# Opposite array halves and two-head products for the sample tile, and its high and low parts as one stationary operand, in a one-core decoder layer

## The chip, the cores and the metric

The kernel runs on one core of a Trainium2 chip. The metric is the device time of one execution in microseconds (us), lower is better. Before the change the median of three runs is 2130.78 us (2129.83 to 2131.91).

## What is computed

One layer of a hybrid decoder for a prompt of 1024 tokens and a sample group of 64 tokens (8 sequences of 8 new tokens, each with 2048 cached tokens), with the same weights, in float32:

```python
h = rmsnorm(x, norm_mix);  proj = h @ w_in            # 1088 rows, D_MODEL = 1024
# head group A: sparse softmax attention, 8 heads x 64, top-k keys chosen by an indexer
# head group B: gated delta rule, 4 heads, d_k = d_v = 128
gc = cumsum(g);  decay = exp(gc_i - gc_j) for i >= j  # per head
u, w = solve(strict(kb k^T * decay) + I, [vb, kb * exp(gc)])
v_new = u - w S;  o = (q * exp(gc)) S + (q k^T * decay) v_new
S = S * exp(g_last) + (k * exp(g_last - gc))^T v_new  # new state, is returned
x = x + concat(o_a, gated rmsnorm(o_b)) @ w_out
x = x + square(relu(rmsnorm(x, norm_mlp) @ w_up)) @ w_down;  final rmsnorm
```

The outputs are the new rows of both groups, the new keys and values, and the new states of head group B: one for the prompt and eight (one for each sample sequence, 4 heads x 128 x 128) for the samples.

## The kernel before

Tokens lie in nine tiles: eight prompt tiles of 128 rows and tile 8 (`NT`) with the 64 sample rows. The kernel is a row of hand-written stages; in each of them every engine has its own list of instructions, ordered by semaphores. A stage in its own block ends with a barrier of all engines and of what the SP queue waits for.

**Gates** (`stage_gates`, inside the block that ends at L1391): TensorE (PE) sums the decays down the tokens (L1430 to L1435), VectorE (DVE) copies them out (L1442, L1443), and PE then sums the squared lengths of the sample heads (L1349), for which DVE waits at L1452.

**Chunks and scan** (`stage_chunks`, one block, 590 to 841 us). The tiles go in pairs (0,1), (2,3), (4,5), (6,7) and the sample tile alone. For every tile:
- DVE multiplies a triangle of ones by the decays into `TG` (L1889), PE multiplies `TG` by a 128x128 matrix of ones into two banks (L1636) and adds a bf16 mask to each (L1637). ScalarE (ACT) takes the exponentials (L1762, L1763).
- PE transposes keys and values (L1631), DVE scales them out of PSUM (L1897 to L1899, semaphore `kept`), PE makes the Gram matrices (L1644, L1646), DVE multiplies them by the decay (L1908, L1909).
- The triangular matrix is inverted in six doubling levels on 64x64 halves (L1659, L1669, L1672, L1683, L1690, with DVE, ACT and GpSimd (POOL) between them), and applied (L1703, L1705). The prompt's recurrence of the pair before (`write_with_state` L1569, `step` L1577 to L1585) is laid between the levels.

With the last pair index (the sample tile) PE also makes the samples' products with their states: eight `unit`s (two products x four heads), each eight matmuls of 128 rows x 64 columns of weights over 128 columns, one for each sequence (L1606). DVE lays each unit's left operand, the sample rows masked by sequence, into one of three buffers (`mask`, L1874). `step(7)` (L1577) follows `unit(3)`, units 4 to 7 follow `step(7)`.

At the end of the block DVE takes the difference from the states (L1971, L1972), copies it masked by sequence, 64 rows x 1024 columns for each head (L1976), and PE makes the update of the eight states in eight products of 64 rows over 512 columns (L1724), one bank each, four banks in turn. DVE finishes the samples' output (L1983 to L2007) and for every product fades half a head's states (L1999) and adds the product (L2001). When all eight are added, SP issues one store of the 2 MB of states (L1560), and the block waits for its landing (L1561). Prompt attention begins in the next block.

**Dense part**: `stage_output_projection` and `stage_mlp` share one block; the projection's lists are run inside the MLP's (L2783, L2822, L2856, L2914). Every float32 product is made of three single-pass products of a high and a low part (`split_product`, L2529 to L2535). The output projection has three groups of three tiles, each over 8 blocks of 128 weight rows; the sample tile is in the last group. Its results are added by DVE (L2722) at the start of the next group, then normed (L2651 to L2708), and the first pieces of the MLP's up product follow the transposes (L2608). The MLP runs over 32 blocks of the hidden width: up products with the 1088 tokens as moving columns in three pieces (L2818), and after every two blocks a down group: nine tiles x two halves of 512 columns x two blocks x three products (L2838), 108 matmuls. The sample tile's hidden columns are a stationary operand of 64 columns there. DVE adds each bank (L2931) and makes the low parts (L2893, L2897, L2912). In the last down group DVE and ACT also do the final norm, tile after tile (L2884 to L2906).

```python
def split_product(pe, out, left, right, start, stop):
    (lh, ll), (rh, rl) = left, right
    pe.matmul(out, lh, rh, start=start, stop=False)
    pe.matmul(out, lh, rl, start=False, stop=False)
    return pe.matmul(out, ll, rh, start=False, stop=stop)
```

## Time and profile before

| | |
|---|---|
| median of 3 runs | 2130.78 us |
| the profiled execution's own time | 2128.11 us |
| its span, first to last instruction | 2126.0 us |
| busy: PE, DVE, ACT, POOL | 90%, 55%, 32%, 12% |
| mean granted TensorE clock | 0.955 of full |

Times in the text are microseconds from the span's start. PE is the matmul row, PEld its weight loads. A matmul's duration includes its way through the array, and matmuls overlap; what one costs in a full queue is the distance from its start to the next start. A float32 matmul that isn't split stands as two instructions. A timeline row merges equal neighbours: start, time from the first start to the last end, engine, line, operation, operands, count, and in brackets the idle time before it with what ended it.

### The profile page before, as it was taken

The page shows a single profiled execution, that of the slowest core. Times are in us where ns is not written, and L with a number is a line of the kernel's source. Part 1 is how long each engine was busy: PE and PEld are TensorE (multiplying, and loading weights), DVE is VectorE, ACT ScalarE, POOL GpSimd, SP SyncE. Part 2 cuts the span into 40 slices and gives each one's busy share as a digit, 9 for nine tenths or more (in the row PEclk, how much of TensorE's full clock was granted, in tenths as well). Part 3 has the DMA queues.
Part 4 walks back from the last instruction along what each step waited for, and adds up shares of the span by engine and source line. Part 5 has one row for each costly group of instructions (what it writes and reads, how often), then busy time and mean ns, then how long its engine had stood idle before and what let it go on. Part 6 is the DMA issues. An engine that isn't in the chain of part 4 may idle for free. (4 is left out here: it accounts for less than half of the span.)

```text
span 2126.0 us, 33335 instructions
## 1 busy us (share of the span) xinstructions
PE 1916.8 (90%) x12648; PEld 1594.5 (75%) x12648; DVE 1176.9 (55%) x2298; ACT 682.0 (32%) x1373; POOL 251.6 (12%) x294
## 2 busy tenths in 40 slices
PE   5999999883488986898999699999999999999998
PEld 5888899883277874566544277888889999988886
DVE  3275578999656546764333266544444444444446
ACT  5332256652423322553322044311111121121113
POOL 4324332210201000001123200000000000000000
PEclk9999999997699996999999899999999999999999
DMA  5324322110110003404899472211111111111102
GB/s 149 83 66 128 88 80 60 30 41 0 51 41 2 2 2 127 176 1 129 280 316 304 127 256 80 79 41 40 40 40 40 41 50 41 40 65 45 40 30 84
DMA packets 121930, 177.33 MB, mean 83 GB/s; under 512 B 33208, under 2 KB 73785, under 8 KB 121644
## 3 DMA queue, kind: packets, MB, share of 16 engines
q1 hardware_dynamic: 104428, 118.05, 17.4%
q0 software_dynamic: 17344, 57.16, 8.6%
q8 instruction: 100, 1.64, 0.3%
q14 instruction: 58, 0.48, 0.1%
HBM read 156.64 MB, written 18.01 MB: 82 GB/s over the span
## 5 line engine op out<-in xcount | busy, mean ns | idle before, releaser
L2533 PE MATMUL banks<-front_h_hi,front_w_hi 128*128 128x364 f32 (+2 forms) x744 | 256.7, 345 | 23.7 <-POOL front_w_lo L627 10.0
L2533 PE MATMUL banks<-h_hi,ml_up_hi 128*128 128x364 f32 (+1 forms) x768 | 252.4, 329 | 1.8 <-DVE h_lo L2708 1.8
L2534 PE MATMUL banks<-h_lo,ml_up_hi 128*128 128x364 f32 (+1 forms) x768 | 252.3, 328 | 0.0
L2535 PE MATMUL banks<-h_hi,ml_up_lo 128*128 128x364 f32 (+1 forms) x768 | 252.3, 328 | 0.0
L2534 PE MATMUL banks<-front_h_lo,front_w_hi 128*128 128x364 f32 (+2 forms) x744 | 249.1, 335 | 0.0
L2535 PE MATMUL banks<-front_h_hi,front_w_lo 128*128 128x364 f32 (+2 forms) x744 | 248.7, 334 | 0.0
L2931 DVE TENSOR_TENSOR x<-x,banks 128x512 f32<-128x512 f32 x256 | 175.7, 686 | 127.3 <-PE banks L2535 127.0
L2533 PE MATMUL banks<-ml_down_hi,ml_hid_hi 128*128 128x512 f32 (+1 forms) x576 | 225.1, 391 | 2.5 <-DVE ml_hid_lo L2912 2.5
L2534 PE MATMUL banks<-ml_down_lo,ml_hid_hi 128*128 128x512 f32 (+1 forms) x576 | 225.1, 391 | 0.0
L2535 PE MATMUL banks<-ml_down_hi,ml_hid_lo 128*128 128x512 f32 (+1 forms) x576 | 224.8, 390 | 0.0
L296 DVE TENSOR_SCALAR_CACHE_REDUCE work<-arena,work 128x384 bf16<-128x384 f32 (+5 forms) x194 | 176.1, 957 | 1.0 <-issue 0.3
L2533 PEld LDWEIGHTS banks<-front_h_hi,front_w_hi 128*128 128x128 f32 (+1 forms) x744 | 142.5, 192 | 41.5 <-POOL front_w_lo L627 11.9
L2941 DVE TENSOR_TENSOR arena<-arena 128x364 f32<-128x364 f32 (+1 forms) x96 | 51.3, 536 | 198.7 <-ACT arena L2871 198.7
L2533 PEld LDWEIGHTS banks<-h_hi,ml_up_hi 128*128 128x128 f32 x768 | 144.3, 188 | 3.4 <-issue 2.0
L2534 PEld LDWEIGHTS banks<-h_lo,ml_up_hi 128*128 128x128 f32 x768 | 144.4, 188 | 0.7
L2535 PEld LDWEIGHTS banks<-h_hi,ml_up_lo 128*128 128x128 f32 x768 | 144.4, 188 | 0.0
L2534 PEld LDWEIGHTS banks<-front_h_lo,front_w_hi 128*128 128x128 f32 (+1 forms) x744 | 142.7, 192 | 0.7
L2535 PEld LDWEIGHTS banks<-front_h_hi,front_w_lo 128*128 128x128 f32 (+1 forms) x744 | 142.4, 191 | 0.9
L2854 ACT CAST ml_down_hi<-arena 128x1024 fp32r<-128x1024 f32 x32 | 32.1, 1048 | 297.7 <-PE banks L2535 293.3
L2533 PEld LDWEIGHTS banks<-ml_down_hi,ml_hid_hi 128*128 128x128 f32 (+1 forms) x576 | 105.1, 182 | 27.7 <-DVE ml_hid_lo L2912 2.8
L2535 PEld LDWEIGHTS banks<-ml_down_hi,ml_hid_lo 128*128 128x128 f32 (+1 forms) x576 | 105.0, 182 | 26.4
L2534 PEld LDWEIGHTS banks<-ml_down_lo,ml_hid_hi 128*128 128x128 f32 (+1 forms) x576 | 105.1, 182 | 25.4
(432 smaller groups left out, 3266.4 us busy)
## 6 DMA issues: line engine op xcount, KB each, us to landing
upper<-in_cache_k SPq DMA_DIRECT2D x128, 256.0 KB, 4.2
upper<-in_cache_v POOLq DMA_DIRECT2D x112, 256.0 KB, 4.4
arena<-in_w_up SPq DMA_DIRECT2D x32, 512.0 KB, 4.2
arena<-in_w_down SPq DMA_DIRECT2D x32, 512.0 KB, 5.7
work<-in_w_in POOLq DMA_DIRECT2D x30, 512.0 KB, 4.6
op_raw<-in_w_out SPq DMA_DIRECT2D x24, 512.0 KB, 3.9
arena<-in_x_prompt SPq DMA_DIRECT2D x8, 512.0 KB, 6.0
upper<-in_cache_v SPq DMA_DIRECT2D x16, 256.0 KB, 4.0
```

The lines of the kernel that those rows point to most:

```text
L296: dve.tensor_scalar(junk, sc[0:rows, :], than, 0.0, op, ALU.add, accum_out=out[0:rows, i:i + 1]).then_inc(self.counted, 1)
L2533: pe.matmul(out, lh, rh, start=start, stop=False)
L2534: pe.matmul(out, lh, rl, start=False, stop=False)
L2535: return pe.matmul(out, ll, rh, start=False, stop=stop)
L2854: act.copy(dhi[:, n % 2, :], raw_down[:, n % 2, :]).then_inc(down_hi, 1)
L2931: dve.tensor_tensor(part, part, k.psum[4 + n % 4][0:r, :], ALU.add).then_inc(added, 1)
L2941: dve.tensor_tensor(tmp[:, j, 0:w], tmp[:, j, 0:w], tmp[:, j, 0:w], ALU.mult).then_inc(squared, 1)
```

## The change

Four edits stand in the diff. The title under which the change came also names the dense part in one block; both kernels have it so already, and the diff holds nothing on it.

1. Decay rows. In the gates stage DVE clears a buffer and copies the summed decays (36 columns: 9 tiles x 4 heads) twice into it, at columns 0 and 64; PE transposes it; DVE copies the result out. So each tile and head has its decays as a row, once in partitions 0 to 35 and once in 64 to 99. `TG` is now those rows times a selection of the tile's four, and the two decay products contract 36 rows each, one in the lower and one in the upper half of the array, one behind the other and ahead of both masks. The sample tile takes both from the lower rows.
2. Units by pairs. `unit(u)` makes heads h and h+1 at once, head h into PSUM partitions 0 to 63 and h+1 into 64 to 127, matmuls alternating; it waits for both masks. There are four mask buffers. `unit(0)` and `unit(2)` come in levels 0 and 1 of the last pair, none in level 2 nor behind the solve; then `unit(4)` and `unit(6)`.
3. State update. The masked copy is 64x512 for each head, the products contract 32 rows each, alternately partitions 0 to 31 and 32 to 63. The fades go to POOL, all eight, behind the last unit. DVE takes each of the two differences in two instructions. The states are stored in four DMAs, one for each head, as soon as it is added.
4. Dense part. The samples' high and low parts lie side by side as 128 columns. One product of both with the weights' high part puts high x high into partitions 0 to 63 and low x high into 64 to 127; a second one of the high part alone with the weights' low part goes to 0 to 63. So two matmuls take the place of three, and DVE adds both halves of the bank, one after the other, with a wait between. The low part of the last token piece is made in two instructions.

```diff
 stage_gates, tensor:
             pe.matmul(k.psum[2][:, 0:DB * G], k.c["ones"][0:NS, :], ...).then_inc(summed, 1)
+            pe.wait_ge(laid, 3)
+            pe.transpose(k.psum[0][0:COPY, P:2 * P], decay_wide, k.c["ident"]).then_inc(rows_turned, 1)
 stage_gates, vector:
             dve.tensor_copy(flat(k.gl), k.psum[1][:, 0:n]).then_inc(base, 1)
+            dve.memset(decay_wide, 0.0).then_inc(laid, 1)
+            dve.wait_ge(laid, 1)
+            for at in (0, HALF):
+                dve.tensor_copy(decay_wide[:, at:at + n], k.psum[0][:, 0:n]).then_inc(laid, 1)
 stage_gates, vector_last:
+            dve.wait_ge(rows_turned, 1)
+            dve.tensor_copy(k.decay_rows[0:COPY, :], k.psum[0][0:COPY, P:2 * P])
 stage_chunks, sync:
-            sp.wait_ge(addS, 2 * G)
-            sp.dma_start(a["new_ssm_sample"][0].rearrange("b h k v -> k (b h) v"), S0).then_inc(out_sem, 16)
-            sp.wait_ge(out_sem, 32)
+            for h in range(G):
+                sp.wait_ge(addS, 2 * (h + 1))
+                sp.dma_start(a["new_ssm_sample"][0, :, h].rearrange("b k v -> k b v"), S0v[:, :, h, :]).then_inc(out_sem, 16)
+            sp.wait_ge(out_sem, 16 * (G + 1))
 stage_chunks, tensor, unit(u):
-                pe.wait_ge(mask_sem, u + 1)
+                pe.wait_ge(mask_sem, u + 2)
                 for b in range(DB):
-                    last = pe.matmul(k.psum[K_STATE if part else Q_STATE][0:NS, h * DK:(h + 1) * DK], state_mask[u % 3][:, b * NS:(b + 1) * NS],
-                                     S0[:, b * G + h, :], start=(b == 0), stop=(b == DB - 1))
-                last.then_inc(with_state, 1)
+                    for i in range(2):
+                        last = pe.matmul(k.psum[K_STATE if part else Q_STATE][i * NS:(i + 1) * NS, (h + i) * DK:(h + i + 1) * DK],
+                                         state_mask[(u + i) % 4][:, b * NS:(b + 1) * NS], S0[:, b * G + h + i, :], start=(b == 0), stop=(b == DB - 1))
+                last.then_inc(with_state, 2)
 stage_chunks, tensor, each pair:
+                    for b, rows in ((2, slice(0, ROWS)), (3, slice(HALF, HALF + ROWS) if t < NT else slice(0, ROWS))):
+                        pe.matmul(bank(s, b, r), k.c["ones"][rows, 0:r], TG[s][rows, :, 0:r], start=True, stop=False)
                     for b, mask in ((2, "low_big"), (3, "up_big")):
                         mask = ...
-                        pe.matmul(bank(s, b, r), k.c["ones"][0:r, 0:r], TG[s][0:r, :, 0:r], start=True, stop=False)
                         last = pe.matmul(bank(s, b, r), k.b["ident"][0:r, 0:r], mask, start=False, stop=True)
...
                     elif l < S_LEVELS:
-                        unit(l)
+                        if l < 2:
+                            unit(2 * l)
                         scan_part(i, l)
...
-            unit(3)
             pe.wait_ge(left[0], 2 * (LAST + 1))
             step(NT - 1)
-            for u in range(G, 2 * G):
+            for u in range(G, 2 * G, 2):
                 unit(u)
...
-                pe.matmul(k.psum[n % 4][:, :], k.KD[NT][0:NS, h, :], vnm[0:NS, h, half * 512:(half + 1) * 512],
-                          start=True, stop=True).then_inc(kvS, 1)
+                rows = slice(half * NS // 2, (half + 1) * NS // 2)
+                pe.matmul(k.psum[n % 4][:, :], k.KD[NT][rows, h, :], vnm[rows, h, :], start=True, stop=True).then_inc(kvS, 1)
 stage_chunks, gpsimd, at its end:
+            pool.wait_ge(with_state, len(units))
+            for n in range(2 * G):
+                ...
+                pool.tensor_tensor(part, part, eg[...].unsqueeze(2).to_broadcast([P, 4, DK]), ALU.mult).then_inc(fadeS, 1)
 dense part:
+def split_product_samples(pe, bank, both, right, start, stop):
+    rh, rl = right
+    if start:
+        pe.matmul(bank, both, rh, start=True, stop=False)
+        return pe.matmul(bank[0:NS, :], both[:, 0:NS], rl, start=False, stop=False)
+    pe.matmul(bank[0:NS, :], both[:, 0:NS], rl, start=False, stop=False)
+    return pe.matmul(bank, both, rh, start=False, stop=stop)
...
+                        if t == NT:
+                            dve.tensor_tensor(part, part, k.psum[4 + n % 4][NS:P, :], ALU.add).then_inc(low_added, 1)
+                            dve.wait_ge(low_added, LOW_BEFORE + 2 * f + i + 1)
                         dve.tensor_tensor(part, part, k.psum[4 + n % 4][0:r, :], ALU.add).then_inc(added, 1)
```

## Rows read from the trace of the kernel before

**Rows 1.** Stretches: length, busy PE, PEld, DVE, ACT, POOL, granted clock, DMA share, GB/s
```profile
590.00:831.00 241.00, 211.78 (x3018) 180.63 (x3018) 144.10 (x283) 68.71 (x222) 18.15 (x26) 0.93 0.06 18
...
1335.00:2126.00 791.00, 779.66 (x4053) 699.74 (x4051) 382.09 (x575) 162.34 (x290) 0.00 (x0) 0.99 0.15 48
```

**Rows 2.** The page's chain that ended last, by engine
```profile
PE 41%; DMA 1%; DVE 1%; ACT 0%; issue 0%; DVEq 0%; ACTq 0%
```

**Rows 3.** Timeline, PE: a down group's last prompt matmul and first sample matmul
```profile
1396.32 0.39 PE L2535 MATMUL banks<-ml_down_hi,ml_hid_lo 128*128 128x512 f32 x1
...
1396.55 0.40 PE L2533 MATMUL banks<-ml_down_hi,ml_hid_hi 128*64 128x512 f32 x1
```

**Rows 4.** Groups by shape: the sample tile's third products, MLP and output projection
```profile
L2535 PE MATMUL banks<-ml_down_hi,ml_hid_lo 128*64 128x512 f32 x64 | 25.0, 390 | 0.0
...
L2535 PE MATMUL banks<-op_w_hi,h_lo 128*64 128x512 f32 x16 | 6.2, 391 | 0.0
```

**Rows 5.** Timeline, 1329 to 1335: from the output projection into the MLP
```profile
1329.38 2.66 DVE L2722 TENSOR_TENSOR x<-x,banks 128x512 f32<-128x512 f32 x4 [0.74 <-PE banks L2535]
...
1332.04 1.38 DVE L2722 TENSOR_TENSOR arena<-arena,banks 64x512 f32<-64x512 f32 x2
...
1334.40 1.09 PE L2608 MATMUL banks<-arena 128*128 128x128 f32 x8 [1.71 <-DVE arena L2693]
```

**Rows 6.** Timeline: the samples' last additions and the final norm behind them
```profile
2118.24 1.45 DVE L2931 TENSOR_TENSOR arena<-arena,banks 64x512 f32<-64x512 f32 x2
...
2119.72 1.02 ACT L2884 ACTIVATE banks<-arena 64x1024 f32<-64x1024 f32 x1 [1.28 <-DVE arena L2931]
```

**Rows 7.** Timeline, PE: a prompt tile's first decay product and mask, the next tile
```profile
628.84 1.02 PE L1636 MATMUL banks<-upper,arena 128*128 128x512 f32 x2
629.70 0.38 PE L1637 MATMUL banks<-arena 128*128 128x512 bf16 x1
...
630.99 1.04 PE L1631 MATMUL banks<-arena,work 128*128 128x128 f32 x8
```

**Rows 8.** Timeline, DVE: the second tile's keys and values start
```profile
632.07 0.69 DVE L1897 TENSOR_TENSOR arena<-banks,work 128x512 f32<-128x512 f32 x1 [1.14 <-PE banks L1631]
```

**Rows 9.** Timeline, PE, prompt attention: neighbours on opposite rows; on opposite columns
```profile
871.41 1.13 PE L2138 MATMUL banks<-work 64*128 64x512 f32 x4
...
919.85 1.15 PE L2173 MATMUL banks<-upper,work 128*64 128x128 f32 x18
```

**Rows 10.** Timeline, PE: the samples' products with their states
```profile
798.63 1.16 PE L1577 MATMUL banks<-arena,upper 128*128 128x128 f32 x8
...
803.69 1.96 PE L1606 MATMUL banks<-upper,work 128*64 128x128 f32 x16 [2.11 <-DVE work L1874]
...
807.23 3.66 PE L1606 MATMUL banks<-upper,work 128*64 128x128 f32 x32
```

**Rows 11.** Masked copies, state products; fades and additions (ns min/median/max, first to last start)
```profile
812.13 4.61 DVE L1976 TENSOR_TENSOR arena<-work,arena 64x1024 f32<-64x1024 f32 x4
...
816.80 13.80 PE L1724 MATMUL banks<-arena,upper 64*128 64x512 f32 x16 [2.91 <-DVE arena L1976]
...
L1999 DVE TENSOR_TENSOR upper<-upper,work x8: 676/688/694, 819.4 to 830.6; 128x512 f32<-128x512 f32 x8
...
L2001 DVE TENSOR_TENSOR upper<-upper,banks x8: 686/686/687, 820.1 to 831.4; 128x512 f32<-128x512 f32 x8
```

**Rows 12.** POOL lines, ns min/median/max: 128x512 with DVE mostly idle, 64x256 beside DVE
```profile
L1173 POOL TENSOR_TENSOR upper<-upper,arena x8: 1252/1253/1272, 568.4 to 577.0; 128x512 f32<-128x512 f32 x8
...
L1816 POOL TENSOR_TENSOR arena<-arena x8: 719/767/812, 604.6 to 732.3; 64x256 f32<-64x256 f32 x8
```

**Rows 13.** DMA issues: count, KB, median us to landing
```profile
out_new_ssm_sample<-upper SPq DMA_DIRECT2D x1, 2048.0 KB, 8.7
...
arena<-in_w_up SPq DMA_DIRECT2D x32, 512.0 KB, 4.2
```

**Rows 14.** Timeline, DVE: the end of the gates, first read of the sample lengths
```profile
586.09 0.16 DVE L1452 TENSOR_SCALAR upper<-banks 128x4 f32<-128x4 f32 x1 [2.58 <-PE banks L1349]
```

More of the change, by code:

```diff
@@ L1416, in stage_gates @@
     k.stat_at = m.take(3 * n)
+    COPY = HALF + n
+    k.decay_rows, decay_wide = k.view(m.take(P), P), k.view(m.take(COPY), COPY)
     assert m.at <= k.split, m.at
@@ L1820, in _ @@
                     pool.tensor_tensor(ZM[s][0:r, G:2 * G, :], TG[s][0:r, :, 0:HALF], wide(ident, r), ALU.add).then_inc(low_made[s], 1)
+            eg = k.eglS.rearrange("p (b h) -> p b h", h=G)
+            pool.wait_ge(with_state, len(units))
+            for n in range(2 * G):
+                h, half = n // 2, n % 2
+                part = S0v[:, 4 * half:4 * half + 4, h, :]
+                pool.tensor_tensor(part, part, eg[:, 4 * half:4 * half + 4, h].unsqueeze(2).to_broadcast([P, 4, DK]), ALU.mult).then_inc(fadeS, 1)
         @block.vector
@@ L1884, in _ @@
                     r = rows_of(t)
-                    tri = k.c["tri" if t < NT else "tri_s"][0:r, 0:r].unsqueeze(1).to_broadcast([r, G, r])
+                    line = k.decay_rows[0:HALF + ROWS, 0:r].unsqueeze(1).to_broadcast([HALF + ROWS, G, r])
+                    own = k.b["ident_half"][0:HALF + ROWS, t * G:(t + 1) * G].unsqueeze(2).to_broadcast([HALF + ROWS, G, r])
                     if i:
@@ L1888, in _ @@
                         dve.wait_ge(low_made[s], 3 * i)
-                    dve.tensor_tensor(TG[s][0:r, :, 0:r], tri, g[0:r, t, :].unsqueeze(2).to_broadcast([r, G, r]), ALU.mult).then_inc(spread[s], 1)
+                    dve.tensor_tensor(TG[s][0:HALF + ROWS, :, 0:r], line, own, ALU.mult).then_inc(spread[s], 1)
                 for s, t in enumerate(pair):
@@ L1941, in _ @@
                         if l == 0:
-                            for u in range(3):
+                            for u in range(4):
                                 mask(u)
@@ L1958, in _ @@
                     sizes(i)
-            mask(3)
             new_state(NT - 1)
@@ L1970, in _ @@
             dve.wait_ge(with_state, len(units))
-            dve.tensor_tensor(k.uS[0:NS], k.uS[0:NS], heads(k.psum[K_STATE])[0:NS], ALU.subtract).then_inc(vn, 1)
-            dve.tensor_tensor(oS[0:NS], heads(k.psum[Q_STATE])[0:NS], wide(k.egc[0:NS, NT, :]), ALU.mult).then_inc(o_steps, 1)
+            two = lambda x: x.rearrange("p (a i) d -> p a i d", i=2)
+            for i in range(2):
+                rows = slice(i * NS, (i + 1) * NS)
+                own = two(k.uS[0:NS])[:, :, i, :]
+                last = dve.tensor_tensor(own, own, two(heads(k.psum[K_STATE]))[rows, :, i, :], ALU.subtract)
+            last.then_inc(vn, 1)
+            fading = k.egc[0:NS, NT, :].rearrange("p (a i) -> p a i", i=2)
+            for i in range(2):
+                rows = slice(i * NS, (i + 1) * NS)
+                last = dve.tensor_tensor(two(oS[0:NS])[:, :, i, :], two(heads(k.psum[Q_STATE]))[rows, :, i, :],
+                                         fading[:, :, i:i + 1].to_broadcast([NS, G // 2, DK]), ALU.mult)
+            last.then_inc(o_steps, 1)
             dve.wait_ge(vn, NT + 1)
@@ L1998, in new_sample_state @@
                 dve.wait_ge(kvS, n + 1)
-                dve.tensor_tensor(part, part, eg[:, 4 * half:4 * half + 4, h].unsqueeze(2).to_broadcast([P, 4, DK]), ALU.mult).then_inc(fadeS, 1)
                 dve.wait_ge(fadeS, n + 1)
@@ L2624, in tensor @@
                             right = whi[:, (g * KD + f) % RING, i * 512:(i + 1) * 512], wlo[:, (g * KD + f) % RING, i * 512:(i + 1) * 512]
-                            last = split_product(pe, k.psum[j][0:rows_of(t), :], left, right, f == 0, f == KD - 1)
+                            if t < NT:
+                                last = split_product(pe, k.psum[j], left, right, f == 0, f == KD - 1)
+                            else:
+                                last = split_product_samples(pe, k.psum[j], k.h_hi[:, f, SEQ:TOK + NS], right, f == 0, f == KD - 1)
                             if f == KD - 1:
@@ L2721, in vector @@
                         dve.wait_ge(made, NP * (g - 1) + j + 1)
+                        if t == NT:
+                            dve.tensor_tensor(part, part, k.psum[j][NS:P, :], ALU.add).then_inc(low_added, 1)
+                            dve.wait_ge(low_added, i + 1)
                         dve.tensor_tensor(part, part, k.psum[j][0:r, :], ALU.add).then_inc(added, 1)
```

47 lines of the change are left out of this document (29 added, 18 removed).

## The prediction, made before the changed kernel was seen

> **What bounds the kernel now.** First the page's chain that ended last [rows 2]: its known part is nearly all PE, and busy time by stretch [rows 1] says the same of the dense part: 779.66 of 791 us with PE busy at a granted clock of 0.99, DVE busy less than half. What leaves PE's queue there leaves the span. In the chunk block (590 to 831) PE is busy 211.78 of 241 us, but in the timeline it stands between steps of DVE and ACT, so each saving has to be followed to the next wait. At the block's end nothing overlaps: masked copies, then state products, then the last addition, begun at 831.4, ended at 832.05 [rows 11], then a store of 8.7 us [rows 13], for which the barrier waits.
>
> **Part 1, the dense part.** Distance between starts, not duration, is the price: 1396.32 to 1396.55, 0.23 us for a 512-column matmul in a full queue [rows 3]. The same for 64 columns of weights as for 128, so a product with both parts side by side costs no more than one with 64. One of three goes: 64 matmuls in the MLP and 16 in the output projection [rows 4].
>
> MLP: a down group's sample tile goes from 12 to 8 matmuls, 0.92 us less. In 15 of the 16 groups that is pure gain, 13.8 us: DVE's two additions more (0.69 us each, half of 1.38 [rows 5]) fit into its idle half [rows 1], and nothing queued behind them on DVE (low parts of weights, squares of the next up product) is needed by PE for several us. In the last group DVE sets the end: its additions run from 2118.24 to 2119.69 and ACT follows at 2119.72 [rows 6]. PE being earlier helps nothing, and four additions instead of two take 2.75 us and some 0.05 for each wait: end +1.3. The low part made in two instructions costs about 0.1 on DVE, covered. **MLP: -12.5 us.**
>
> Output projection: 16 x 0.23 = 3.7 us less. Seven of the eight blocks give theirs, 3.2. In the eighth DVE is the path: four prompt additions from 1329.38, the samples' from 1332.04 to 1333.42, then the norm that PE waits 1.71 us for [rows 5]. PE's earlier end helps nothing there, and two additions more come ahead of that norm, +1.4. The start of the projection waits for weights, unchanged. **-1.8 us.**
>
> The Trainium skill speaks against this edit: TensorEngine Tiling (Array Packing), "Key Properties", says that changing the tiling mode, not just the tile, drains TensorE. The trace disagrees so far: from a 128*128 to a 128*64 matmul the distance is the same 0.23 us [rows 3]. What a drain would do is a rival below.
>
> **Part 2, decay products.** One product over 512 columns is two instructions, 628.84 to 629.70, 0.86 us; with its mask and the second pair the tile takes 628.84 to 630.99, 2.15 us [rows 7]. Neighbours on opposite rows overlap: four instructions over 512 columns took 1.13 us [rows 9], two took 1.02 [rows 7]. So the two products cost about what one does, and I take 0.83 us less for a tile, 1.65 for a pair. It reaches the end of the pair: the Gram products that follow wait for the second tile's keys and values, on DVE from 632.07 on, three instructions of some 0.65 [rows 8]; with everything 0.8 earlier these are ready at about 633.0, and by then PE is on the first tile's Gram products. Three pairs: 5.0 us. Pair 0 starts at a half granted clock, where the first tile saves up to twice that: 2.0 us. Products over 36 rows aren't in the trace; bounds are no overlap (0) and 2 x 0.86 for four pairs plus the slow start (-8). I take **-7.0**, nearest to rows 9. The sample tile keeps both products on the same rows: 0. DVE's `TG` has the same 512 elements: 0.
>
> **Part 3, gates.** PE's sums of the sample lengths, for which DVE waits 2.58 us and ACT and the block's end after it [rows 14], now stand behind a transpose that waits for DVE: a clear and two copies of 36 columns (small DVE instructions, 0.16 [rows 14]), two handovers, and the transpose. **+1.2 us** (bounds +0.5, +2). The copy of the transposed rows lies in DVE's wait for ACT: 0.
>
> **Part 4, the last pair and the samples' end.** Two units in a row cost 803.69 to 807.23, 1.77 us each, and 1.9 with the change from another shape [rows 10]. Heads on opposite columns overlap: 18 instructions of that shape took 1.15 us in prompt attention [rows 9] against 1.96 for 16 here [rows 10]. So a pair of units costs one. Step by step, against the profiled times:
> - `unit(0)` waits for a second mask: +0.6. Levels 0 and 1 now carry two heads in the time of one; the unit in level 2 and the one behind the solve go: -3.8. Part of it is lost: `step(7)` also waits for ACT's copies of the solve (`left`), by the timeline about 1.4 us. `step(7)` starts not at 798.63 but at about 796.8: -1.8.
> - Units 4 to 7: PE began 2.11 us late, at 803.69, for the first mask, and ended at about 810.8 [rows 10]. It now waits for two masks (+0.6) and needs 3.8 instead of 7.1 us. End at about 806.3: -4.5 in all. DVE's gates of the last two prompt tiles (L1862, by the timeline 2.2 us) now end later than this, at 806.7; the differences, four instructions of half width, end at 808.2.
> - Masked copies: 4.61 us for four of 1024 columns [rows 11]; for 512 columns about half and a small fixed part, 2.45 us. End at 810.6, was 816.7: -6.1.
> - State products: eight took 13.8 us, 1.72 each, at half clock [rows 11]. On opposite 32-row parts neighbours overlap; each then costs 0.86 at half clock, 0.43 at full. DVE takes over as the bound: the output steps ahead of the first fade are 2.7 us (816.7 to 819.4), then come eight additions of 0.69 which overlap to 0.64, and 0.8 for two last output steps. 810.6 + 2.7 + 5.1 + 0.8 = 819.2, was 832.05: **-12.8 us**. POOL's fades start at 806.3: 1.25 each alone [rows 12], the last at 816.3, before its addition at 818.6. Beside DVE's two-input instructions a POOL line took up to 812 ns at half that size and less [rows 12], 1.5 in place of 1.25 if scaled from its 665: 818.3, just in time. Bounds: -9 (no overlap of 32-row parts at a half clock) and -15.
> - Store: the last DMA is a quarter; 512 KB in the same pieces took 4.2 us [rows 13]. The others were issued 1.2 us apart before it, less than the 1.7 each needs of bandwidth (8.7 for all), so the queue delays the last a little: 4.7 in place of 8.7, **-4.1 us** (bounds 0, -4.5).
>
> **Sum.** -12.5 - 1.8 - 7.0 + 1.2 - 12.8 - 4.1 = -37.0 us. The profiled execution's own time is 2128.11 us (span 2126.0), so 2091.1; the median of the runs stands 2.7 higher, so **2093.8 us**. Attention, between the two regions, has no edit; its start at a half clock is taken as before.
>
> **Rivals.**
> - **A drain at each change of width.** By this rule's mechanism an alternation of 128 and 64 columns empties the array: 0.16 us each (0.39 duration less 0.23 [rows 3]). The new order has two changes for each half in a down group and four for each block in the projection, 96, where 48 were. +7.7 us: 2101.5. Against it: entering the sample tile costs nothing in rows 3. For it: that entry comes once a group. 8%.
> - **Small products don't overlap** (36 or 32 rows, semaphores between state products). Parts 2 and 4 lose the decay gain and most of the products': 7.0 and about 4 us. 2105. For: neither shape is in the trace. Against: rows 9. 7%.
> - **Slower than before: the clock.** At the entry of the MLP PE now stands 3.5 us instead of 1.71 [rows 5]. If the granted clock fell to half there and stayed, PE would lose half of that stretch. 74 us at half clock use up the gain, 83 decide for slower; 110 us would give 2093.8 + 55 = 2148.8. Against: that stretch was at 0.99 over 791 us [rows 1] with the wait of 1.71 in it, and PE is full behind it. 2%.
> - **Nothing changes much** because the shortened parts meet waits that I haven't seen, as ACT in the last pair or the early loads of the next block. 3%: 2128.
> - "Dense part in one block" isn't in the diff: 0.
>
> **The numbers.** Forecast 80%. Its own terms add up to -21 with every unseen cost at its weak bound and -41 with every one at its strong bound, 2109.5 and 2089.5; half of the weak side is likelier than all of it, and it takes in the first rival. Below, another 3 us for attention's start, which ran at a half clock behind a wait that now is shorter. Range 2086 to 2104. A measurement here tells about 0.2%, 4.3 us, from no change. Faster by more 95%, within 3%, slower 2%.
>
> **What would show it.** Down groups with 104 matmuls and 0.23 us from start to start also between widths; the end 1.3 us later behind the last matmul. The decay products of a tile within about 1.1 us, the next transposes 1.3 us after them. Units in pairs of 1.9 us, the last ended at about 800.5 (806.3 less the 5.8 of parts 2 and 3); the last addition some 19 us before 832, the next block's first matmul some 23 before 841. Wrong would be: DVE or POOL as releaser of PE inside the MLP, POOL's fades releasing DVE's additions, a longer half-clock stretch behind 1330, or state products 1.7 us apart.

## The result, and the profile after

Changed kernel: 2103.34 us median of 4 runs (2100.89 to 2104.93), before 2130.95 in the same session; ratio 0.9874, 95% interval 0.9862 to 0.9886. That is 27.6 us less where the forecast said 37.0, and only 0.7 us inside the upper end of the range. Two further series of the same kernel (below) gave ratios of 0.9891 and 0.9877, 25.1 and 27.2 us less; one execution of the first of them took 3751.36 us, and all its figures here are of the other four. The profiled execution took 2104.93 us.

First the page after, its slices of PE and granted clock (each slice is 52.6 us).

```profile
span 2102.9 us, 33268 instructions
PE 1892.0 (90%) x12569; PEld 1585.7 (75%) x12569; DVE 1199.2 (57%) x2370; ACT 682.5 (32%) x1373; POOL 262.6 (12%) x302
PE   5999999985479886998999699899999999999997
PEclk9999999997679987999999899999999999999999
```

The dense part is as full as before. In the chunk block (slices 12 to 16) PE reads 7 9 8 8 6 where it was 8 8 9 8 6, and the clock 7 9 9 8 7 where it was 9 9 9 9 6: lower in the block's first slice and in the one with the last pair (736 to 789). Next, the two stretches of [rows 1], in the same columns, at their new places.

```profile
594.00:825.00 231.00, 197.06 (x3018) 169.38 (x3018) 141.34 (x278) 69.01 (x223) 28.99 (x34) 0.92 0.08 24
1323.00:2100.00 777.00, 766.05 (x3980) 695.75 (x3978) 403.81 (x636) 161.87 (x290) 0.00 (x0) 0.99 0.15 49
```

PE has some 15 us less to do in the chunk block, DVE 3 less, POOL 11 more (the fades). To find where the time went I laid the traces side by side by the starts of the same instructions. Microseconds in each stretch; "changed" is the range of its three traces:

```
stretch                                            before  changed        forecast of   measured
                                                                          the change    (mean)
gates: first sum to first transpose of the block    10.1   11.1             +1.2        +1.0
to the last Gram product of the sample pair        180.9   174.0 to 174.2   -7.0        -6.8
to the last state product of step(7)                28.4    30.6 to 30.7    -1.8        +2.3
to the end of the last addition                     32.5    26.0 to 27.2   -11.0        -6.1
to the next block's first matmul                     9.1     4.7            -4.1        -4.4
output projection, first product to third up        119.9   119.9 to 121.5  -1.8        +0.9
MLP, from there to the last norm                    775.9   763.7 to 765.2  -12.5       -11.2
```

The seven add up to -37.0 and -24.3. (Where the kernel before has one trace only, two of the single parts below stand beside it for the projection: 119.9, 121.2 and 121.4 without the dense edit, 120.8 in the mean, as with it. So the +0.9 is none.) The rest of the span carries no edit and scatters: start to gates took 576.6 to 583.6 us in the traces of this study, prompt and sample attention, up to the projection's first product, 382.6 to 388.9. So one execution says little of 2 us; a stretch says more: four of the seven repeat within 0.3 us over the three traces, the other three within 1.6. The forecast failed most in three stretches: last pair, samples' end, and output projection with the boundary to the MLP.

**Dense part.** Timeline, PE after: the last sample tile.

```profile
2091.44 0.39 PE L2571 MATMUL banks<-ml_down_hi,ml_hid_hi 128*128 128x512 f32 x1
2091.66 0.40 PE L2572 MATMUL banks<-ml_down_lo,ml_hid_hi 128*64 128x512 f32 x1
2091.90 0.39 PE L2573 MATMUL banks<-ml_down_lo,ml_hid_hi 128*64 128x512 f32 x1
2092.13 0.39 PE L2574 MATMUL banks<-ml_down_hi,ml_hid_hi 128*128 128x512 f32 x1
```

Starts are 0.22 to 0.24 us apart across each change of width, as in [rows 3]. Timeline after, 1313 to 1320, the rows that answer to [rows 5]:

```profile
1313.15 2.65 DVE L2769 TENSOR_TENSOR x<-x,banks 128x512 f32<-128x512 f32 x4 [0.29 <-PE banks L2563]
1315.84 0.69 DVE L2767 TENSOR_TENSOR arena<-arena,banks 64x512 f32<-64x512 f32 x1
...
1318.00 0.68 DVE L2769 TENSOR_TENSOR arena<-arena,banks 64x512 f32<-64x512 f32 x1
...
1319.67 1.97 PE L2648 MATMUL banks<-arena 128*128 128x128 f32 x8 [3.65 <-DVE arena L2737]
```

The wait in front of tile 6's transposes grew from 1.71 to 3.65 us, and the eight transposes take 1.97 instead of 1.09: the granted clock has fallen to half (1.2 of 2.4 GHz) at 1318.0 for 6.8 us.

**Decay.** Timeline, PE after, one prompt tile, to be set beside [rows 7]:

```profile
632.37 1.13 PE L1649 MATMUL banks<-upper,arena 36*128 36x512 f32 x4
633.43 0.60 PE L1652 MATMUL banks<-arena 128*128 128x512 bf16 x2
633.87 1.04 PE L1645 MATMUL banks<-arena,work 128*128 128x128 f32 x8
```

From the products to the masks are 1.06 us, to the next tile's transposes 1.50, and 0.10 more than before pass ahead of the products, at the change of shape: of the 2.15 us of before a tile gives 0.55.

**The samples' end.** Timeline after, DVE, POOL and PE, to be set beside [rows 10] and [rows 11]:

```profile
807.31 0.84 DVE L1996 TENSOR_TENSOR work<-work,banks 64x256 f32<-64x256 f32 x2
...
808.96 5.25 DVE L2007 TENSOR_TENSOR arena<-work,arena 64x512 f32<-64x512 f32 x4
...
817.04 0.99 DVE L2021 SCALAR_TENSOR_TENSOR work<-work 64x4 f32<-64x4 f32 x1
```
```profile
807.16 10.86 POOL L1841 TENSOR_TENSOR upper<-upper,work 128x512 f32<-128x512 f32 x8 [34.94 <-PE banks L1620]
```
```profile
803.36 1.97 PE L1620 MATMUL banks<-upper,work 128*64 128x128 f32 x32 [2.71 <-DVE work L1895]
805.15 1.92 PE L1620 MATMUL banks<-upper,arena 128*64 128x128 f32 x32
...
814.26 3.78 PE L1740 MATMUL banks<-arena,upper 32*128 32x512 f32 x8 [4.19 <-DVE arena L2007]
818.69 5.17 PE L1740 MATMUL banks<-arena,upper 32*128 32x512 f32 x8 [0.64 <-DVE upper L2029]
```

Units in pairs take 1.8 us and state products overlap, as forecast. But four masked copies of half the size take 5.25 us, more than the 4.61 of the full size.

**The last pair.** Timeline, PE: `unit(0)`, one head, in the kernel before; `unit(0)` and `unit(2)`, two heads each, after. The granted clock is at half from 772.7 to 779.5 before, and from 768.4 to 778.7 and 782.1 to 788.9 after.

```profile
776.69 3.31 PE L1606 MATMUL banks<-upper,work 128*64 128x128 f32 x16 [1.65 <-DVE work L1874]
```
```profile
774.16 3.68 PE L1620 MATMUL banks<-upper,work 128*64 128x128 f32 x32 [2.25 <-DVE work L1895]
...
783.76 3.68 PE L1620 MATMUL banks<-upper,arena 128*64 128x128 f32 x32
```

### The profile page after: what moved, and what is told of

Same layout as the page of the kernel before. It is cut to its first block and busy times, and to the rows that moved or that the text cites. A ratio compares the mean times of both kernels' runs of the same rounds, so it can differ in the third digit from the quotient of the medians.

```text
span 2102.9 us, 33268 instructions
## 1 busy us (share of the span) xinstructions
PE 1892.0 (90%) x12569; PEld 1585.7 (75%) x12569; DVE 1199.2 (57%) x2370; ACT 682.5 (32%) x1373; POOL 262.6 (12%) x302
## 5 line engine op out<-in xcount | busy, mean ns | idle before, releaser
L2561 PE MATMUL banks<-ml_down_hi,ml_hid_hi 128*128 128x512 f32 x512 | 199.9, 390 | 2.5 <-DVE ml_hid_lo L2967 2.5
L2562 PE MATMUL banks<-ml_down_lo,ml_hid_hi 128*128 128x512 f32 x512 | 200.0, 391 | 0.0
L2563 PE MATMUL banks<-ml_down_hi,ml_hid_lo 128*128 128x512 f32 x512 | 199.9, 390 | 0.0
L2923 ACT ACTIVATE arena<-banks 128x364 f32<-128x364 f32 (+1 forms) x96 | 45.3, 474 | 230.1 <-PE banks L2563 230.1
L2561 PEld LDWEIGHTS banks<-ml_down_hi,ml_hid_hi 128*128 128x128 f32 x512 | 96.5, 189 | 22.4 <-DVE ml_hid_lo L2967 2.8
L2563 PEld LDWEIGHTS banks<-ml_down_hi,ml_hid_lo 128*128 128x128 f32 x512 | 96.5, 189 | 20.2
```

The costliest lines, as they stand in the source:

```text
L2923: act.activation(tmp[:, j, 0:w], k.psum[n % 4][:, 0:w], ACT.Relu).then_inc(relued, 1)
```

## The experiments

### The three parts alone

Each is the kernel before with one part of the diff: dense (side by side parts), decay (gates and decay products), samples (units, fades, state products, stores). The changed kernel ran beside them, and once more at the end.

> The kernel before with the dense edit alone (high and low parts of the samples side by side; decay, gates and sample states as before). The forecast's terms give 14.3 us less than before (12.5 in the MLP, 1.8 in the output projection). The reading of the trace after gives less: the 80 matmuls are gone at 0.23 us each, but at the boundary PE waits 3.65 us instead of 1.71 and the granted clock halves behind the wait (about 2.4 us lost, 1.4 more at 1335), so about 10 less. If the clock there was chance, about 13. A drain at each change of width would leave 6 to 7.

> The kernel before with the decay edit alone (rows of the transposed sums on opposite halves, with the transpose in the gates). The forecast's terms give 5.8 us less than before (7.0 less 1.2). The trace after gives 1.1 us for each of three pairs, 0.3 for pair 0, and 1.1 back in the gates: about 2.5 less. In the trace a tile should take 1.5 to 1.6 us from its products to the next transposes, 2.15 before.

> The kernel before with the sample part alone (units in pairs, fades on POOL, state products on opposite rows, four stores). The forecast's terms give 16.9 us less than before (12.8 and 4.1). The trace after gives 1.8 for each pair of units at full clock, masked copies of 5.3 instead of 2.45 us, and two more stretches at a half granted clock in the last pair: 9 to 12 less. If the half clock in the last pair was chance, its trace has no such stretches and it comes to 12 or more.

> The changed kernel itself, as the yardstick for the three parts. If the parts don't touch each other, its gain is the sum of the three (by the forecast 37, by the reading of the trace 22 to 27); if a part's gain depends on another (the clock, transfers that start earlier), it differs from the sum by more than 3 us.

> The changed kernel once more, beside both_mended: 2103 to 2106, 24 to 27 us below before, with the same half-clock stretches from 767, 781, 811, 1317 and 1330 on.

```
              ratio to before    interval           us
dense         0.9942             0.9926 to 0.9958   -13.0 (medians)
decay         0.9984             0.9973 to 0.9995    -3.0
samples       0.9973             0.9962 to 0.9984    -5.9
after_again   0.9891             0.9874 to 0.9907   -25.1
after_third   0.9877             0.9856 to 0.9899   -27.2
```

The trace of the third series has the same half-clock stretches in the last pair, at the same steps of the program (from 762.5 and 776.2, in an execution that reached the chunk block 5 to 6 us earlier), and one more of 3.4 us at 796.6, with which its stretch to the last addition is the longest, 27.2 us for 26.0 in the other two; the one expected near 1330 it lacks. The parts add up to 21.9, and within the intervals that is the whole's gain: no effect of one part on another can be told. The dense part is worth nearly what was forecast (14.3), decay half (5.8), the samples' part a third (16.9), and less than the 9 to 12 us expected for it after the first trace. Its own trace has two further half-clock stretches of 3.4 us, at 802.1 and 808.9, where step(7) and the units behind it run, and from step(7) to the last addition it takes 28.4 us. The sharpest reading is the third stretch of the table above, from the sample pair's Gram products to step(7): 28.4 us in dense as before, but 31.0 in decay and 30.2 in samples. Decay changes no instruction in there (its products end ahead of it), and yet loses 2.6 us. Stretch 760 to 800, PE busy and granted clock, in before, decay, samples and the changed kernel:

```profile
760.00:800.00 40.00, 32.52 (x274) 0.87 0.00 1
```
```profile
760.00:800.00 40.00, 32.60 (x259) 0.83 0.00 1
```
```profile
760.00:800.00 40.00, 31.12 (x299) 0.79 0.01 1
```
```profile
760.00:800.00 40.00, 31.00 (x266) 0.79 0.00 1
```

The clock is what differs. In decay it is at half for 10.2 us from 768.9, just behind the last prompt pair; in before for 3.4 us from 762.4 and 6.8 from 772.7.

### The fades: where POOL meets DVE

fades_dve puts them back on DVE, fades_act makes them 32 ACT instructions (the diff is shortened).

```diff
-            for n in range(2 * G):        # POOL, behind unit 7
-                pool.tensor_tensor(part, part, eg[...], ALU.mult).then_inc(fadeS, 1)
+            fade_sample_state(len(units) - 2, 0)      # ACT: heads 0 and 1, behind units 4 and 5
+            keep_output(NT - 2); keep_output(NT - 1)
+            fade_sample_state(len(units), G)          # heads 2 and 3
```

> The changed kernel with the eight fades of the sample states on ACT (32 instructions of 128x128) instead of POOL. If POOL's fades hold DVE's masked copies back, the four copies take about 2.5 us instead of 5.25, the output steps behind them some 0.6 less, and the span is 2.5 to 3.5 us below the changed kernel's. If the copies are slow for their own form (64x512 from two SBUF operands), they stay at 1.3 us each and the time doesn't move.

> The changed kernel with the fades on DVE as before, ahead of each addition. If POOL's fades hold DVE back, the masked copies take 2.5 us (2.8 less), the output steps 0.6 less, and the eight fades of 0.65 us come on top of the additions (up to 5.2 more, less where the additions now wait for PE): within 2 us of the changed kernel, so moving them to POOL brought little. If they don't, it is about 5 us slower than the changed kernel.

The copies in fades_act, and PE's wait behind them:

```profile
804.51 2.48 DVE L2013 TENSOR_TENSOR arena<-work,arena 64x512 f32<-64x512 f32 x4
```
```profile
806.51 0.63 PE L1609 MATMUL banks<-arena,work 128*128 128x128 f32 x4 [3.12 <-ACT arena L1756]
807.07 1.74 PE L1732 MATMUL banks<-work,upper 64*64 64x128 f32 x8
```

Without POOL beside them the copies take 2.48 us, the forecast's 2.45, in both kernels (fades_dve too). So POOL's fades held them back: 5.25 for 2.48 is shown, and the fades went from 1.0 to 1.1 us at the start of their row to 1.45 beside the copies and the steps behind them. The Trainium skill, SBUF — State Buffer, "SBUF: two separate sides", has the mechanism: GpSimd and a VectorE instruction with two SBUF inputs take one port pair in turn, each for its whole length. The trace agrees: copies and fades alternate, both 1.45 us from start to start, where a copy alone takes 0.6; the additions behind them, which read one operand from PSUM, keep their 0.67. Yet the whole gained little. In fades_act PE's transposes of tile 7 wait 3.12 us for ACT's copy, which stands behind the first 16 fades, and so does the sample's `AQ` product (L1732) behind them: step(7) to last addition 25.6 us instead of 26.0; ratio 0.9872 (0.9853 to 0.9891). This trace has the extra half-clock stretch of the third series (at 797.1), beside whose 27.2 us it gains 1.6. In fades_dve the stretch is 27.1 us; ratio 0.9879 (0.9861 to 0.9898). So by one trace, set beside the two of the changed kernel with the same clock, moving the fades from DVE to POOL was worth 1.1 us, where eight instructions of 0.68 seem to promise 5.4. In the whole time the three places for the fades can't be told apart.

### The last pair

units_single takes the heads of units 0 to 3 one by one again, at their old places; early_unit fills two waits that the timeline shows.

```diff
+                if i == LAST:            # PE, behind the Gram products: 2.57 us of waiting there
+                    unit(0)
...
-                        if l < 2:
-                            unit(2 * l)
+                        if l == 1:
+                            unit(2)
...
+                if i == LAST:            # DVE, ahead of the samples' keys
+                    mask(0); mask(1)
```

> The changed kernel with the four units of the last pair one head at a time again and at their old places (levels 0 to 2 and behind the solve); units 4 to 7 stay in pairs. If the pairs of units bring the half granted clock between 768 and 789, that stretch is at 0.87 as before, each unit takes 1.8 us, step(7) starts 2 to 3 us earlier than in the changed kernel, and the time is about 2 us lower. If the clock falls there anyway, single units at half clock cost 3.6 us each and the time is 4 us or more higher.

> The changed kernel with masks 0 and 1 made in DVE's wait ahead of the samples' keys, and the first pair of units placed behind the Gram products, where PE waits 2.57 us for DVE, instead of at level 0, where it waits 2.26 us for the masks. If PE's idle time there is what brings the half granted clock from 767 on, the stretch 760 to 800 rises above 0.79 and step(7) starts 5 us or more earlier than in the changed kernel; if the clock falls as before, the order alone gives about 3 us.

units_single: ratio 0.987 (0.9852 to 0.9889), the stretch 31.0 us, granted clock 0.83 with 10.2 us of half clock from 768.8: single units cost up to 3.6 us each there. So the pairs of units don't bring the half clock. The first expectation fell; the second was too high, as the second half-clock part lasted 3.4 us instead of 6.8. early_unit: ratio 0.9861 (0.9829 to 0.9893). From Gram products to step(7) 24.2 us, 6.5 less than the changed kernel, and the timeline shows the first pair of units at full clock:

```profile
766.96 1.91 PE L1620 MATMUL banks<-upper,work 128*64 128x128 f32 x31
```
```profile
760.00:800.00 40.00, 31.66 (x289) 0.85 0.13 43
```

The 10.2 us of half clock that began at 767 are gone, 6.8 from 774.2 remain. (The second pair of units still ran at half, 3.68 us.) But two stretches of 3.4 us appear at 791.2 and 798.1; in the first of them eight products of step(7) take 1.86 us instead of 1.06, and of the 6.5 us 3.2 are given back before the last addition. The order changed here together with the wait, so this doesn't show the cause of the half clock.

### The order at the end

tail moves masks 4 to 7 around the last new state, the gates of the last two prompt tiles and their transposes behind the sample additions, and has the fades on ACT: four changes in one (the diff is shortened).

```diff
+            mask(G); mask(G + 1)
             new_state(NT - 1)
+            mask(G + 2); mask(G + 3)
             output(NT - 1)
-            for u in range(G, 2 * G):
-                mask(u)
-            sizes(LAST); inverses(LAST); gate(NT - 2); gate(NT - 1)
...
             for i in range(1, G):
                 new_sample_state(i)
+            inverses(LAST); gate(NT - 2)
             for i in range(G, 2 * G):
                 new_sample_state(i)
+            gate(NT - 1)
```

> The changed kernel with masks 4 to 7 around the last new state, the fades on ACT, and the gates of the last two prompt tiles with their transposes behind the sample additions. The run with the fades on ACT gave copies of 2.5 us but lost the gain where PE waited for ACT's copies behind the fades (first state product 1.74 us after the copies). If that order was the loss, the last addition comes about 20 us after step(7)'s state product, instead of 26, and the time is 4 to 6 us below the changed kernel's; if the end is bound by state products at half clock and additions, at most 2 us.

Ratio 0.9847 (0.983 to 0.9864), 32.6 us below before. Step(7) to last addition: 22.2 us, not 20. DVE stood still once more, for a root on ACT that is queued behind the 32 fades:

```profile
813.45 0.17 DVE L2042 RECIPROCAL work<-work 64x4 f32<-64x4 f32 x1 [2.51 <-ACT work L1828]
```

### The boundary to the MLP

scale_first puts the norm of tile 6 ahead of the samples' additions; samples_first has PE and DVE treat the samples first in the projection's last block; proj_three gives the projection its three products back; wait_filled adds work that nobody reads, where PE waits:

```diff
+                    if (g, f) == (NG, 1):
+                        pe.wait_ge(kept, 2 * GT * (NG - 1))
+                        for n in range(15):
+                            pe.matmul(k.psum[NP], k.h_hi[:, n % KD, 0:P], whi[:, n % RING, 0:512], start=True, stop=True)
```

> The changed kernel with the norm of tile 6 (scale) ahead of the samples' four additions in the last round of the output projection. The wait of PE at the boundary falls from 3.65 us to about 1.2. If the half clock behind it (1318 and 1335) comes of that wait, it goes too and the MLP's start is 5 to 6 us earlier than in the changed kernel; if it doesn't, 2.4 us.

> The changed kernel with the samples' products first in the last block of the output projection, and their four additions first behind it, so that these run beside the prompt tiles' products. PE's wait at the boundary goes from 4.06 (start to start) to about 2, and no addition stands between scale and keep of tile 6. If the half clock behind the boundary is due to PE standing still there, the 14.0 to 15.2 us from tile 6's transposes to the third up product go back to 12.4, as in the kernels without the dense edit; in all 3 to 4 us. If the clock isn't tied to it, only about 2 us.

> The changed kernel with 15 products of 512 columns, whose result nobody reads, in the wait of PE at the boundary between output projection and MLP (15 x 0.23 = 3.4 us in a wait of 3.65). If PE standing still brings the half clock at the MLP's entrance, it is gone: from tile 6's transposes to the third up product 12.4 us instead of 14.0 to 15.2, and the span 2 us or so shorter. If the clock has another reason, the stretch stays at 14 or more and nothing is gained.

> The changed kernel with three products for the samples in the output projection again (MLP as changed). The projection's products take 3.5 us more (about 106 instead of 102.5), the wait at the boundary is 2.11 again instead of 4.06, and if the half clock hangs on that wait the 14.0 to 15.2 us behind it are 12.4: in all within 1 us of the changed kernel, so that the projection's share of the edit is worth nothing. If the clock doesn't hang on the wait, it is about 1.6 us slower.

```
                       products    wait   tile 6's transposes to third up   ratio (interval)
before, decay, samples 105.4-106.8 2.11   12.42-12.43
dense, changed (3)     101.9-103.2 4.06   13.8-14.8
scale_first            101.9       1.53   15.9                              0.9887 (0.9868-0.9907)
samples_first          101.8       3.97   14.0                              0.9874 (0.9856-0.9893)
proj_three             105.5       2.11   12.43                             0.9894 (0.9875-0.9912)
wait_filled            103.4       4.06   12.42                             0.9871 (0.9852-0.9890)
```

(Waits from start to start.) wait_filled settles it. PE with its 15 products, and both stretches to the third up product, of wait_filled and of the changed kernel:

```profile
1316.95 3.56 PE L2676 MATMUL banks<-op_w_hi,h_hi 128*128 128x512 f32 x15
1320.78 1.09 PE L2648 MATMUL banks<-arena 128*128 128x128 f32 x8 [0.27 <-DVE arena L2741]
...
1320.78:1333.20 12.42, 10.58 (x72) 1.00 0.00 1
```
```profile
1319.67:1334.45 14.78, 12.94 (x72) 0.83 0.00 1
```

The same instructions after the same 4.06 us, 12.42 us at full clock when PE had worked through the wait, 14.78 at 0.83 when it had stood still. scale_first only moves the standstill: 1.53 us ahead of the transposes, then 2.9 from their start until the first up product (0.86 before), which needs all additions; and its clock fell too. samples_first changes nothing either: the eight additions stand in one queue on DVE, with the samples' four now ahead of tile 6's, whose norm waits for them all the same. And proj_three shows what the projection's share of the edit is worth: 3 to 4 us of products, given for a wait longer by 2 and a stretch behind it longer by 1.4 to 2.4. Nothing. In the whole time the 2 us of wait_filled can't be told from the scatter. A second, shorter stretch of half clock (3.4 us) stayed in both wait_filled (at 1333.5) and proj_three (at 1333.0), so it doesn't hang on this wait.

### The price of two products on opposite rows

rows64 lets both decay products run over 64 rows instead of 36.

```diff
-    for b, rows in ((2, slice(0, ROWS)), (3, slice(HALF, HALF + ROWS) if t < NT else slice(0, ROWS))):
+    for b, rows in ((2, slice(0, HALF)), (3, slice(HALF, P) if t < NT else slice(0, HALF))):
```

> The changed kernel with the decay products over 64 rows each (zeros above row 36) instead of 36. In the trace after, the two overlapping products of 512 columns take 1.06 us at full clock, where one alone took 0.86. If the number of rows matters (a part of 32 rows that isn't filled), 64 rows change the 1.06; if it is the price of two overlapping products as such, it stays at 1.06 and the time is the changed kernel's.

```profile
631.33 1.13 PE L1649 MATMUL banks<-arena 64*128 64x512 f32 x4
632.39 0.61 PE L1652 MATMUL banks<-arena 128*128 128x512 bf16 x2
```

1.06 us again; ratio 0.9881 (0.9864 to 0.9897). The number of rows is not what makes it 1.06. In this one trace the half clock at the start of the block lasted 3.4 us less than in the changed kernel's three, and the first pair of tiles was 2.0 us faster than in the kernel before, which is what the forecast gave it.

### What the parts of the answer give together

block_moved is tail and early_unit with the samples' last reciprocal behind four additions; block_moved_three has three products in the projection as well; both_mended is block_moved with wait_filled's 15 products.

> The order of tail and of early_unit together, and the samples' last reciprocal behind four additions instead of one (DVE stood 2.51 us there for ACT's root). From the last pair's Gram products to step(7) 24 us (30.6 in the changed kernel), from there to the last addition about 20 (26.0). By waits alone next block's first product comes 10 to 12 us earlier than in the changed kernel; if half clock follows wherever PE is less busy, 6 to 8. Median about 2094 to 2097.

> block_moved with three products for the samples in the output projection. Within 1 us of block_moved if the projection's share of the dense edit is worth nothing; 1.6 us slower if the half clock at the MLP's entrance stays.

> block_moved together with the 15 products in the wait at the boundary. block_moved alone stood at 2091.4; from tile 6's transposes to the third up product 12.4 us instead of 14.0: about 2089.5, some 40 us below before, 13 below the changed kernel. If the clock's two causes aren't independent, no more than block_moved.

```
                     median us   ratio     interval
block_moved          2091.40     0.9826    0.9810 to 0.9843
block_moved_three    2092.54     0.9818    0.9796 to 0.9839
both_mended          2092.43     0.9819    0.9799 to 0.9839
changed, beside it   2104.12     0.9877    0.9856 to 0.9899
```

All three beat both kernels: 37 to 39 us below before; both_mended is 11.7 below the changed kernel that ran beside it. In block_moved the Gram products to step(7) take 24.2 us (24 expected) and from there to the last addition 22.0 (20 expected); the next block's first matmul comes 10.7 us earlier after the block's start than in the changed kernel's first trace. Gain and new order come together here: no run says which of the moved steps brought how much. The projection's two ways are equal, as expected; both_mended has its stretch of 12.42 us, and in the total that doesn't show.

## Why the prediction was right or wrong

The forecast's sum was 12.7 us too good in the stretches. The samples' end had 4.9 of it, the last pair 4.1, the projection 2.7 by these traces (1.8 if its +0.9 is taken as none), the MLP 1.3.

**MLP, -12.5 forecast, -11.2 measured.** Right in every mechanism: 104 matmuls in a down group, DVE's additions covered, four additions instead of two at the end. No drain between widths: that rival (+7.7) fell, and here the trace disagrees with the rule of the Trainium skill, TensorEngine Tiling (Array Packing), "Key Properties", as to this change of columns. One trace gives -12.2, the other two -10.7: these have 3.4 us of half clock from 1330 or 1335 on, which the third and the kernel before lack.

**Output projection, -1.8 forecast, nothing measured.** Its terms were right: the products take 3.7 us less (102.6 for 106.3, means of three traces), the wait grows by 1.9, of which 0.5 is PE's earlier end and 1.4 the two additions. What failed is that nothing stood behind the wait. The clock falls there and costs 1.4 to 2.4 us, which is what was left. The forecast had this as its rival for slower, but asked for 83 us of half clock; it came for 3.4 to 6.8 us at a time.

**Decay, -7.0 forecast, -6.8 in its stretch, and that is luck: the step was wrong.** "I take 0.83 less for a tile" sets the 1.13 us of [rows 9] beside the 1.02 of [rows 7], both with the last instruction's tail; from start to start one product is 0.86, two in a row would be 1.72, and the overlapping pair is 1.06. A tile gives 0.55, a pair 1.1, three pairs 3.3. Pair 0, taken at 2.0, gave 0.2 to 0.3: its half clock lasted 3.4 us longer than before. What fills the sum to 6.8 are two half-clock stretches of 3.4 us, at 714.7 and 762.4 in the trace before, which dense and samples have too and no kernel with the decay edit has; each was worth 1.6. In the sample pair 2.6 us come back as half clock, so that the part alone is worth 3.0.

**Gates, +1.2 forecast, +1.0 measured.** Right.

**Last pair, -1.8 forecast, +2.3 measured.** The wait for `left` came as named (0.94 us ahead of step(7), with 0.34 for DVE shortly before it 1.3 for the 1.4 forecast), and 0.6 for the second mask (2.25 us ahead of `unit(0)`, 1.65 before). The failing step is to cost the units at the full clock of [rows 10], and the rest of PE's work at its old price. From start to start `unit(0)` and `unit(2)` took 3.6 us each, at half clock, where the single units in their places had taken 3.2 (at half already, which the forecast passed over) and 1.9: 2.1 us. The products between them, up to step(6), ran at half as well and took 1.9 us more.

**Samples' end, -11.0 forecast after step(7), -6.1 measured.** The step was "4.61 us for four of 1024 columns; for 512 columns about half": 2.48 without POOL, 5.25 with it. The forecast did see that POOL's instructions get longer beside DVE [rows 12] and priced that on POOL's side; it did not price it on DVE's, which was the path. The output steps lost 1.0 more in the same way, 3.7 instead of 2.7, one of them a 64x4 instruction that took 0.99 instead of 0.15 us. The last additions then wait for state products at half clock (0.37 and 0.42 us). The three add up to 4.6 of the 4.9 us that were missed. What the fades on POOL saved was 1.1 us, by one trace.

**Store, -4.1 forecast, -4.4 measured.** Right: four stores of 512 KB, the last one alone behind the last addition.

The second rival, small products that don't overlap, fell: products of 36 and of 32 rows do overlap. So did "slower" and "nothing changes much".

Shown by a change of one thing are: the copies' price (fades_act, fades_dve), the half clock at the MLP's entrance (wait_filled, and again in both_mended). That a new order at the block's end gains is shown by tail and block_moved, which move several steps at once. Only argued is why the half clock of the sample pair grew: units_single excludes the pairs of units, early_unit, with a wait filled and the order changed, moves it, but decay alone brings it as well, and no run there kept all else equal. What brings the short stretch from 1330 or 1335 on stays open; it was there with the wait filled too.

## What to carry to other kernels

When an edit takes work off TensorE in a stretch where it already waits, price what remains at half clock as well, and look for work to put into the wait: a new order of the engines' steps gave another 11 us here. When work moves to POOL, price it on VectorE's side too, for each instruction beside it that reads two operands from SBUF. And read the price of an overlap from start to start in a row that has the overlap, not from the price of one.

## What the runs showed of the hardware that was not expected

Two products on opposite rows take 1.06 us at full clock where one takes 0.86, whether over 36 or 64 rows. At half clock the overlap is free: eight instructions of 32 rows in 3.78 us, two in every 0.85, where sixteen of 64 rows took 13.8 one by one, 0.86 each [rows 11]. Two on opposite columns cost nothing extra at either: 1.79 us from start to start for 32 instructions where 16 took 1.77 [rows 10], 3.6 at half clock where 16 took 3.6 in units_single.

PE standing still for 3.65 us between full stretches was followed by half clock in the stretch behind it, in all of the twelve traces that have this wait unfilled (13.8 to 15.2 us for 12.4), and in none of the seven where it was 1.71 us or filled. scale_first, with its standstill in two parts, had it too. Fifteen products that nobody reads made the work behind them shorter.
